# One 1 MB expert load issued in the mixing stage instead of after routing, and new homes for three small operands

## The reference, cut to what matters

```python
x = x + jnp.concatenate([y_conv, y_lru], axis=-1) @ w_out[i]
hf = _rmsnorm(x, g_ffn[i]).reshape(B * S, D)
eid, gate = _hier_route(hf, w_group[i], b_group[i], w_expert[i], b_expert[i])
x = x + _routed_experts(hf, eid, gate, w1[i], w3[i], w2[i]).reshape(B, S, D)
...
y = (jax.nn.silu(xb @ w1[e]) * (xb @ w3[e])) @ w2[e]
```

## Time and profile before

| what | us |
|---|---|
| median of 3 runs (lowest, highest) | 1229.04 (1226.81, 1230.04) |
| profiled execution, its own time | 1228.61 |
| its span, first to last instruction | 1227.0 |
| PE busy in the span | 1190.4 (97%) |
| DVE busy | 673.6 (55%) |
| ACT busy | 504.2 (41%) |
| bytes moved by DMA | 394.98 MB, mean 322 GB/s |

### The profile page before, as it was taken

One profiled execution on the slowest core, in us unless ns is written; L12 is line 12 of the kernel. 1 busy time (PEld: TensorE's weight loads), 2 busy tenths in 40 slices (PEclk: granted clock), 3 DMA queues, 4 the chain that ended last, 5 costly groups with the idle time before them and its releaser, 6 DMA issues.

```text
span 1227.0 us, 16442 instructions
## 1 busy us (share of the span) xinstructions
PE 1190.4 (97%) x6522; PEld 817.3 (67%) x6522; DVE 673.6 (55%) x1206; ACT 504.2 (41%) x779; POOL 53.8 (4%) x103
## 2 busy tenths in 40 slices
PE   6899999999999999999999999999999999999997
PEld 2597688888889877888878786445444444554436
DVE  5599979787889787755466675111211121121126
ACT  1479663344565576443447384111112111111125
POOL 0100001000010000001001100000000000000000
PEclk9999999999999999999999999999999999999999
DMA  9996868887846555856457779999999999999991
GB/s 366 382 351 271 324 211 334 323 319 293 329 162 242 177 228 185 315 189 230 175 224 261 256 303 427 427 425 426 425 426 426 425 428 424 429 423 427 425 421 44
DMA packets 50987, 394.98 MB, mean 322 GB/s; under 512 B 6673, under 2 KB 8913, under 8 KB 11378
## 3 DMA queue, kind: packets, MB, share of 16 engines
q1 hardware_dynamic: 39618, 337.18, 68.5%
q0 software_dynamic: 9072, 53.92, 12.4%
q10 hardware_dynamic: 2240, 3.10, 1.0%
HBM read 390.68 MB, written 3.49 MB: 321 GB/s over the span
## 4 chain that ended last, share of the span: by engine, by line
PE 81%; DVE 8%; DMA 6%; ACT 3%; SPq 1%; issue 1%; DVEq 0%; ACTq 0%
PE psum L1417 16%; PE psum L794 10%; PE psum L787 10%; PE psum L790 10%; PE psum L1460 8%; PE psum L1349 4%; DMA w_odd_next<-in_w 3%; PE psum L860 2%; PE psum L864 2%; PE psum L862 2%; PE psum L1357 2%; DMA w_raw<-in_units 2%; DVE w_parts L2168 2%; PE psum L821 1%; PE psum L1112 1%; PE psum L1124 1%
## 5 line engine op out<-in xcount | busy, mean ns | idle before, releaser
L2168 DVE TENSOR_TENSOR w_parts<-w_raw,w_parts 128x2048 fp32r<-128x2048 f32 x106 | 241.7, 2288 | 69.3 <-ACT w_parts L1550 69.3
L1550 ACT ACTIVATE w_parts<-w_raw 128x2048 fp32r<-128x2048 f32 x106 | 202.2, 1912 | 79.1 <-DMA w_raw<-in_units 79.1
L1417 PE MATMUL psum<-slabs,arena 128*64 128x512 f32 x704 | 196.3, 592 | 1.0 <-DMA w_odd_late<-in_w 1.0
L787 PE MATMUL psum<-w_parts,h_parts 128*128 128x512 f32 x392 | 155.6, 397 | 3.9 <-ACT h_parts L1550 3.7
L790 PE MATMUL psum<-w_parts,h_parts 128*128 128x512 f32 x392 | 153.3, 391 | 0.0
L1550 ACT ACTIVATE arena<-psum 128x512 f32<-128x512 f32 (+1 forms) x59 | 30.0, 510 | 293.3 <-PE psum L1436 140.6
L1417 PEld LDWEIGHTS psum<-slabs,arena 128*64 128x64 f32 x704 | 62.9, 137 | 110.5 <-issue 108.5
L794 PE MATMUL psum<-w_parts,h_parts 128*128 128x512 f32 x392 | 106.1, 393 | 0.1
L2151 DVE CUSTOM_DVE_ANT_0 aring<-aring,cb 128x1024 f32<-128x1024 f32 x80 | 94.6, 1219 | 0.7 <-DMA aring<-in_ada 0.6
L787 PEld LDWEIGHTS psum<-w_parts,h_parts 128*128 128x128 f32 x392 | 73.9, 188 | 20.8 <-issue 3.2
L1417 PE MATMUL psum<-w_odd,arena 128*64 128x512 f32 x192 | 85.1, 593 | 0.4 <-DMA w_odd_next<-in_w 0.4
(11 more groups left out here) (340 smaller groups left out, 1922.9 us busy)
## 6 DMA issues: line engine op xcount, KB each, us to landing
w_raw<-in_units SPq DMA_DIRECT2D x110, 1024.0 KB, 5.1
slabs<-in_w SPq DMA_DIRECT2D x22, 2048.0 KB, 21.5
slabs<-in_w SPq DMA_DIRECT2D x44, 1024.0 KB, 17.1
aring<-in_ada POOLq DMA_DIRECT2D x40, 1024.0 KB, 5.4
arena<-in_w SPq DMA_DIRECT2D x16, 2048.0 KB, 20.6
w_odd<-in_w SPq DMA_DIRECT2D x16, 2048.0 KB, 20.2
w_odd<-in_w SPq DMA_DIRECT2D x24, 1024.0 KB, 24.3
staged<-in_ada SPq DMA_DIRECT2D x8, 1024.0 KB, 18.5
```

Source lines behind the costliest of these rows:

```text
L787: mm(psum[:, bank, :], high(tile, tok), w_hi(k)[:, col:col + 512], start=first and bank not in begun, stop=False, skip_group_check=True)
L1417: ins = nc.tensor.matmul(psum[s * CAP:(s + 1) * CAP, w, :], xe_t[:, kt, s * CAP:(s + 1) * CAP], up_weights(w, s, b, kt), start=kt == 0, st ...
L1550: return nc.scalar.activation(out_ap, in_ap, func, **kw)
L2168: v.tensor_tensor(w_lo(k), raw(k), w_hi(k).bitcast(F32), ALU.subtract).then_inc(w_split, 1)
```

## The change

One load is issued at another place: the first load of `w3_odd_next` moves on SP from behind `rank_mm` to ahead of the unit `WOUT_AT + 2`, behind a new wait for the fourth `conv_out`. For that, what lies under it must be dead earlier. The vectors used late (`conv_ln_g`, `conv_ln_b`, `lru_w`, `lru_b`) move to the front of `vec`, of which 192 bytes are now kept; `ones_r` is made in place over `ones`, later on ACT; the product of the router's weights with the norm's gain moves on DVE from the first layer to the mixing stage and is written to `w_routed` in the router's scratch. The bytes loaded in all are the same.

```diff
-VECS = [("g_ple", KT), ("g_ffn", KT), ("g_mix", KT), ("b_ada", 96), ("ln_g", 32), ("ln_b", 32), ("subln_g", 1),
-        ("conv_b", 4), ("conv_ln_g", 4), ("conv_ln_b", 4), ("lru_w", CT * LRU_W), ("lru_b", 4),
-        ("b_r", 4), ("b_i", 4), ("lam", 4)]
+VECS = [("g_ple", KT), ("g_ffn", KT), ("conv_ln_g", 4), ("conv_ln_b", 4), ("lru_w", CT * LRU_W), ("lru_b", 4),
+        ("g_mix", KT), ("b_ada", 96), ("ln_g", 32), ("ln_b", 32), ("subln_g", 1),
+        ("conv_b", 4), ("b_r", 4), ("b_i", 4), ("lam", 4)]
...
+        cst_from = place[0]
         cst = kept("cst", [P, 2 * P])
+        ones_r = at("ones_r", cst_from / 1024 + 0.5, [P, P], F32R)
...
-        ones_r = w_forget_parts[:, :, :, :].rearrange("p a k n -> p (a k n)")
...
-        vec_kept = 4 * 2 * KT
+        vec_kept = 4 * 48
...
+        w_routed = rt[:, 108:396].rearrange("p (k n) -> p k n", k=KT)
...
             load_w1_tile(0, 1, 0)
+            sp.wait_ge(conv_ready, CT)
+            load_w3_half(1, 1, 1, 0)
             load_unit(WOUT_AT + 2)
...
             for c in range(2):
                 load_w2(1, 1, c)
-            sp.wait_ge(rank_mm, 1)
-            load_w3_half(1, 1, 1, 0)
...
-                    ins = mm(psum[:, t, 0:36], h_f[:, kt, t * P:(t + 1) * P], w_route[:, kt, :],
+                    ins = mm(psum[:, t, 0:36], h_f[:, kt, t * P:(t + 1) * P], w_routed[:, kt, :],
...
             A(tri_r[:], rc[:, RC_TRI:RC_TRI + P], Cp).then_inc(route_consts, 1)
-            A(ones_r, ones, Cp).then_inc(route_consts, 1)
...
             A(rstd[:], half(5, 0), ACT.Sqrt, scale=1.0 / 512, bias=eps_rms).then_inc(conv_act, 1)
+            A(ones_r[:], ones, Cp).then_inc(route_consts, 1)
...
-                    if layer == 0 and g == 6:
-                        v.tensor_tensor(w_route[:], w_route[:], V("g_ffn", 0, KT).unsqueeze(2).to_broadcast([P, KT, 36]),
-                                        ALU.mult).then_inc(route_consts, 1)
...
+            v.tensor_tensor(w_routed, w_route[:], V("g_ffn", 0, KT).unsqueeze(2).to_broadcast([P, KT, 36]),
+                            ALU.mult).then_inc(route_consts, 1)
             split(Z_AT + 6)
```

More of the change, by code:

```diff
@@ L228, in build @@
         head_sq = kept("head_sq", [P, 4, 8])
-        vec_kept = 4 * 2 * KT
+        vec_kept = 4 * 48
+        assert VEC_AT["g_mix"] <= 48
         w3_odd_next = at("w3_odd_next", (vec_from + vec_kept) / 1024, [P, UNIT])
@@ L274, in build @@
         r_rank = by_tile(236, NE + 2)
-        r_first, r_work, r_el = by_tile(304, NE), by_tile(368, NE), by_tile(432, NE)
-        r_ghot, r_gwork, r_pen = by_tile(496, NG), by_tile(504, NG), by_tile(512, NG)
-        r_s = rt[:, 528:576].rearrange("p (n a) -> p n a", a=TT)
+        w_routed = rt[:, 108:396].rearrange("p (k n) -> p k n", k=KT)
+        r_first, r_work, r_el = by_tile(396, NE), by_tile(460, NE), by_tile(524, NE)
+        r_gwork, r_pen = by_tile(588, NG), by_tile(596, NG)
+        r_s = rt[:, 604:652].rearrange("p (n a) -> p n a", a=TT)
         def hf_t(t, kt):
@@ L1387, in _ @@
             mm(psum[:, 1, 64:64 + NE], tri_r[:], hot_m[:, 1, :], start=True, stop=False)
-            mm(psum[:, 1, 64:64 + NE], ones_r, hot_m[:, 0, :], start=False, stop=True)
-            mm(psum[:, 1, 128:128 + NE], ones_r, hot_m[:, 0, :], start=True, stop=False)
-            mm(psum[:, 1, 128:128 + NE], ones_r, hot_m[:, 1, :], start=False, stop=True).then_inc(rank_mm, 1)
+            mm(psum[:, 1, 64:64 + NE], ones_r[:], hot_m[:, 0, :], start=False, stop=True)
+            mm(psum[:, 1, 128:128 + NE], ones_r[:], hot_m[:, 0, :], start=True, stop=False)
+            mm(psum[:, 1, 128:128 + NE], ones_r[:], hot_m[:, 1, :], start=False, stop=True).then_inc(rank_mm, 1)
             for t in range(TT):
```

## The result

The changed kernel takes 1229.74 us, the median of 21 runs (1226.92 to 1232.02). The kernel before, timed beside it, takes 1227.60 us (21 runs, 1226.41 to 1230.04). The ratio is 1.0014 with a 95% interval of 1.0008 to 1.0020: slower by some 2 us, where a gain of 1.67 us, to 1227.0, was forecast. That is within the 0.3% that was named as what can hardly be told, but it points the other way. The profiled execution of the changed kernel took 1232.02 us with a span of 1230.4, the longest of its runs; its span stands against 1227.0 of before, and the 3.4 us between them can be followed through the rows.

The account below looks back on a forecast made before the run. In the expert stage PE runs full while loads are slower by 2.4 us a pair, surfacing in the last pair. The terms -1.77 and +0.1 sum to -1.67 us: 1228.61 to 1226.94, stated as 1227.0, range 1225.0 to 1229.6.

Parts of the forecast that it names:

- The step that failed: Queue of loads: a lead of at least 2.34 us was to leave no gap, so later landings come 2.46 us sooner.
- Both terms of the sum: Load taken out of the full stretch, -1.77 us at the last pair; load put in ahead of `WOUT_AT + 2`, +0.1 us.
- The output unit, forecast +0.1: Mixing stage: the added 1 MB fits the queue's gap, so `WOUT_AT + 2` lands at 723.42 against 723.34; bounds 0 and +2.46.
- the output unit comes late: Rival, mixing stage: added load misses the gap, `WOUT_AT + 2` lands 2.46 us later, delaying the experts; 1229.3 us, chance 0.06.
- The sign named for it: Changed profile: ACT's split of `WOUT_AT + 2` 6 us or more after its issue means the late unit; about 4.9 was forecast.
- The drained queue in 717 to 720: Ahead of `WOUT_AT + 2`: DMA nearly idle (33, 0, 49 GB/s), taken as room hiding the 1 MB and evidence against a late unit.
- The estimate of +0.9: Alternative for the output unit from about 2.0 us fixed cost per transfer: data start at 719.5, not 718.6; sum -0.9, set aside.
- The last pair, forecast -1.77: End of the expert stage: earlier landings remove PE's waits for `w_odd_late` and `w_odd_next`, -1.77 us; bounds 0 and -2.46.
- The homes, forecast 0: Moved `ones_r` copy, moved gain product and operands read from other places were to cost 0, covered by existing waits.
- the cover named for the DVE product: DVE, ahead of `split(Z_AT + 6)`: 0.71 us idle time until 684.31 was to hide the 0.45 us product; without cover +0.45.
- The gain is lost in a gap: Rival: a 2.87 us lead is not enough, the queue runs dry, the last pair waits as now; 1228.7 us, chance 0.13.
- PE held up by more than the profile shows: Rival, last pairs: slow runs owe their time to later landings, so the whole 2.46 us returns; 1226.7 us, chance 0.15.

Follow-up runs that it names:

- e5: The changed kernel plus 12 unused matrix products on PE while it waits for the last output unit's low part; 1229.81 us, ratio 1.0006 to before.
- e6: The changed kernel again, unaltered; 1230.97 us, ratio 1.0027 to the kernel before.
- e2: The changed kernel with the moved load directly behind `WOUT_AT + 2` and `w_odd_late`, ahead of the last output unit; 1226.89 us, ratio 0.9990 to before.
- e4: The changed kernel with the moved load issued ahead of the 2 MB tile of W1, no longer waiting for `Z_AT + 7`; 1226.94 us, one run.
- e9: e4 again, timed beside the kernel before; 1227.17 us, ratio 0.9991.
- e10: e2 again, timed beside the kernel before; 1227.33 us, ratio 0.9991.
- e7: The changed kernel, but SP issues the output unit only after the added load has landed; 1231.86 us, one run.
- e1: The changed kernel with the moved load back at its old place, only the operands' new homes kept; 1227.95 us, ratio 0.9993 to before.
- e3: The changed kernel with the moved load behind the last output unit and the half of W3 after it; 1227.63 us, ratio 0.9998 to before.

## Why the prediction was wrong, step by step

**The step that failed** is one sentence: "so the queue stays full if the transfer ahead lands at least 2.34 us after the next issue". Both terms of the sum hang on it, and it rested on one pair of rows. A lead is here the time from an issue to the landing of the transfer ahead of it. At two of the three places to which the sentence was applied the runs show:

| place | lead | landing behind the transfer ahead, by the sentence | measured |
|---|---|---|---|
| unit `WOUT_AT + 2` in the changed kernel | 2.64 | 2.46 | 4.66 |
| the same in e5 and e6 | 2.71, 2.76 | 2.46 | 4.58, 4.76 |
| third pair's first load, where the unit was on time (e2, e4, e9, e10) | 2.89, 3.24, 2.67, 2.64 | 2.46 | 4.02, 3.56, 3.36, 3.92 |
| third pair's first load, in the changed kernel (766.31) | 2.01 | - | 5.15 |

At the third, the tile issued near 793 us, the leads are 3.4 us or more instead of the 2.87 that was worked out, and with the load moved it came at most 0.5 us late.

Could the trace of before have told? Six 1 MB transfers of SP, from 150 us to the last pair, have a lead between 2.4 and 3.3 us there, and five of them came 1.5 to 4.5 us late. But these five say nothing of the lead: beside each of them another queue, with loads that GpSimd issues, moved 0.8 to 1.2 MB between the issue and the landing. The unit at 220.83 is one of the five; the unit at 354.98 is the sixth, which had no such company and came 2.54 us behind the transfer ahead, without a gap. Below are issue and time to landing (KB, us) of both, and for 220.83 to 228.40 and for 354.98 to 359.94 the packets, MB and share of each queue (q1 is SP's, q0 the other):

```profile
220.83 0.33 SPq L500 DMA_DIRECT2D w_raw<-in_units  x1
...
w_raw<-in_units SPq DMA_DIRECT2D x1, 1024.0 KB, 7.6
...
q1 hardware_dynamic: 229, 1.61, 57.3%
q0 software_dynamic: 144, 1.05, 35.9%
...
354.98 0.33 SPq L500 DMA_DIRECT2D w_raw<-in_units  x1
...
w_raw<-in_units SPq DMA_DIRECT2D x1, 1024.0 KB, 5.0
...
q1 hardware_dynamic: 262, 1.88, 99.3%
```

All twelve profiles together hold 44 such transfers. Where the other queue moved 0.07 to 0.36 MB beside them (10), none came more than 0.35 us late; where it moved 0.59 to 1.23 MB (18), all came 0.7 to 4.5 us late. The 16 that had no such company split by place: of nine units at 332 to 355 us eight came at most 0.4 us late, and all seven at the two places in the table came 0.9 to 2.3 us late. So the sentence would have passed a look at the undisturbed units of the earlier stages, and failed each time at such leads where it was used. Longer leads were safe: of the 96 transfers with 4 to 6 us, one came 1.5 us late (in e10, beside 1.56 MB of the other queue) and no other more than 0.6. And, as e4 shows with 1.36, the lead alone does not decide; nor is a 1 MB transfer directly ahead (D2) needed for a gap, as the third pair's first load stands behind one of 2 MB.

What happens in such a gap shows in the packets. They carry no engine's number, but joined end to start they give 16 strings, and a packet of 4 bytes closes each string's share of a transfer. Where a string stops, its end cannot be joined to one start for certain, so the strings are given in groups (us):

```
changed,  4 strings:  go from the added load to the unit with no stop over 0.03
changed, 10 strings:  end the added load 718.03 to 718.84, go on 718.48 to 719.30
changed,  2 strings:  end it last, 719.51 and 719.68, go on only 721.09 and 721.13
before,  all 16:      end the 2 MB tile 716.6 to 718.2, go on 719.5 to 720.3
```

The Trainium skill, DMA: Bandwidth & Descriptors, section Why a DMA increments its semaphore by 16 and not by 1, says that a transfer runs on up to 16 engines that finish independently, and counts as landed when all have. The strings agree: fourteen had ended their share of the unit by 722.19, and the two others set its landing at 724.81. In e5 and e6 it is fourteen and two again. Why some restart at once and two only 1.4 to 1.6 us after their last byte was not found, so the cause stays open there; the order of the loads brought it back in every profile of the changed order, and the other order (e4, e9) never did.

**The output unit, forecast +0.1, measured +2.5.** The named rival "the output unit comes late" is what happened, at its price of 2.46; its mechanism was another, since the added load landed at 720.15, well ahead of the 722.6 from which the rival was to decide. That its time of 1229.3 lies near the measured 1229.74 is partly luck: it counts on 1.77 us at the last pair that did not come, and leaves out the clock. The sign named for it, a split of the unit 6 us or more after its issue, was a good one: it starts 7.3 us after (724.83 against 717.51). "The drained queue in 717 to 720" was free for the bytes, but in before all 16 strings restarted within 0.8 us behind it, and in the changed kernel they did not. The estimate of +0.9 that was worked out from the skill's fixed cost lay on the right side and was too small as well. The page gives that cost for transfers issued by GpSimd, and SP's rows differ: in e7 the unit's first packets move at 720.5, a microsecond after its issue at 719.56, and in before the last string begins 1.8 us after the issue, while the landing follows the last packet by 0.4 us.

**The clock, not in the sum, +1.6.** The text passed delays on from ACT to DVE to PE "undiminished". A PE that had waited 2.7 us also came back at 1.2 GHz. The Trainium skill, TensorE: Matmul & The Clock Gate, section Part 1: The HAM clock gate, puts 426.7 ns between the starts of products of 512 columns at this level; the 0.43 us here agree.

**The last pair, forecast -1.77, measured +0.3.** The waits of PE for `w_odd_late` and `w_odd_next` were the right place: over all versions the expert stage takes 419 us and the sum of these two waits (420.47 - 1.31, 420.79 - 1.62 and 420.50 - 1.33 are all 419.2). But the term was too large, and lost besides. Too large: the best versions take 419.3, a gain of 1.2, since the wait of 0.4 us for `w_odd_next` comes back in each. Lost: first in gaps like those that the failed step called seamless. Besides the unit's and the third pair's, the changed kernel has one at the 2 MB tile that is issued at 748.22: it lands 7.70 us behind the transfer ahead at a lead of 2.63, where a tile in the full queue takes 4.9. Second in something not thought of: the transfers need not land evenly. In e10 the last `w_odd` and `w_odd_late` are issued at 1126.52 and 1130.10, and both land 35.5 us later:

```profile
1126.52 3.40 SPq L510 DMA_DIRECT2D w_odd<-in_w  x1
1130.10 3.48 SPq L510 DMA_DIRECT2D w_odd_late<-in_w  x1
```

So they land 3.6 us apart where their price is 2.46; in the trace of before they land 2.5 apart. In the changed kernel it is 3.9:

```profile
1129.45 3.67 SPq L510 DMA_DIRECT2D w_odd<-in_w  x1
1133.31 3.48 SPq L510 DMA_DIRECT2D w_odd_late<-in_w  x1
```

Against the start of the experts, the last `w_odd` lands 1.1 us earlier in both than before, and `w_odd_late` is then 1.1 to 1.4 us later behind it: for e10 that makes 0.0, for the changed kernel +0.3, which are the differences of the third stretch. This unevenness begins at one load between 804 and 827 us and comes back at every later `w_odd_late`, with nothing idle between to even it out. That it is the same lag of single strings as at the unit is likely, but in a full queue the packets can't be told apart, so it stays open.

**The homes, forecast 0,** were right (e1). So was the cover named for the DVE product: it stands at 679.98 with 0.45 us in e1, and DVE's idle time before its next wait for ACT shrinks from 0.71 to 0.34 us.

**The rivals.** "The gain is lost in a gap" held, with the late unit on top: both rivals at once, which the text had priced apart, with chances of 0.13 and 0.06. "PE held up by more than the profile shows" found no support. The spread of the runs goes with the clock: of the runs of before beside e1, 21 with a mean granted clock of 0.998 took 1227.4 us on average, seven with 0.997 1228.8, and five with 0.996 1230.3. No run separates what the clock costs there from what made it fall.

**What stays open:** from the issue of the unit on, the profiled run of the changed kernel is 4.4 us worse than that of before (4.11 + 0.32), the medians only 2.1 and 3.7. The unprofiled runs show no landings, so it isn't known in how many of them the unit is late. Set apart by their mean clock, the runs of the changed kernel take 1229.3 us at 0.998 (8 runs) and 1230.5 at 0.997 (6), against 1227.4 and 1228.8 for those of before beside e1: 1.7 to 1.9 us more at one clock, on several chips' runs and so only roughly.

## What to carry to other kernels

Filling a gap in a queue of loads is not free because the bytes fit into it: here the gap was also where the strings that ran ahead and those that lagged started level again. A threshold for such a queue that was worked out from two rows has to be tried at the place where it will be used: at 332 to 355 us of these traces it passed in eight cases of nine, at the two places of the change it failed each time. And before a late landing is put down to its lead, look at whether another queue moved bytes beside it. Put a prefetch behind the load that the critical path waits for, not in front of it (e2, e3), and price a delay on TensorE's path with what the lower clock adds.

## What the runs showed that was not expected

- Issuing a 1 MB load 2.55 us earlier, to a queue that was still busy, brought its landing forward by 0.17 us (e7 against the changed kernel); behind another order of the same bytes a load with only 1.36 us of lead lost nothing against an idle queue (e4: 4.8 us from issue to landing).
- An uneven landing of two neighbours (3.6 and 3.9 us apart instead of 2.5) lasted for over 300 us of a full queue at 425 GB/s, so it shows in no rate by stretch.
- Of twelve profiles six have a fall to 1.2 GHz between the first 20 us and the tail, at 57 (e5), 146 (before), 740 (the changed kernel, e6, e7), 755 (e1) or 764 us (e5 again), each of 3.4 us but the one at 57 (6.8). The fall at 740 and the one at 755 cost 1.6 us each, about what the change was to bring; the one at 146 cost at most 0.4. The four waits of PE over 2.5 us in that time (2.7, 2.9 and 2.9 us ahead of 740, 4.3 us ahead of 57) were each followed by a fall; the wait of 1.7 to 1.8 us near 142 us, which every profile has, was followed by one in before alone.
